# Turning the residual for the MLP: three of four column blocks by VectorE and device memory instead of TensorE

## The reference

```
x = x + mix @ w_out                       # w_out 2048 x 2048
u = relu(rms_norm(x, norm2_g) @ w_up)     # w_up  2048 x 8192
return x + square(u) @ w_down             # w_down 8192 x 2048
```

## Time and profile before

| | us |
|---|---|
| median of 3 runs (lowest, highest) | 1754.01 (1753.78, 1754.36) |
| the profiled execution's own time | 1757.45 |
| its span, first to last instruction | 1755.6 |
| PE busy | 1744.9 (99%) |
| DVE, ACT, POOL busy | 898.7, 669.1, 207.1 |

### The profile page before, as it was taken

One profiled execution on the slowest core, in us unless ns is written; L12 is line 12 of the kernel. 1 busy time (PEld: TensorE's weight loads), 2 busy tenths in 40 slices (PEclk: granted clock), 3 DMA queues, 4 the chain that ended last, 5 costly groups with the idle time before them and its releaser, 6 DMA issues.

```text
span 1755.6 us, 27160 instructions
## 1 busy us (share of the span) xinstructions
PE 1744.9 (99%) x9270; PEld 1582.7 (90%) x9270; DVE 898.7 (51%) x1718; ACT 669.1 (38%) x1256; POOL 207.1 (12%) x286
## 2 busy tenths in 40 slices
PE   9999999999999999999999999999999999999999
PEld 7999998899997789999888999888999888999887
DVE  5634776666677645454344454344444334545333
ACT  5323754444354444333332333333333333333332
POOL 3301010002352210110000110000111000111000
PEclk9999999999999999999999999999999999999999
DMA  7675469998798554444344444334443434444442
GB/s 182 189 181 149 122 163 222 197 202 217 198 258 261 152 142 115 125 121 130 121 131 120 128 122 123 129 124 127 121 130 120 131 120 130 121 122 129 141 147 96
DMA packets 381393, 261.54 MB, mean 149 GB/s; under 512 B 92444, under 2 KB 328156, under 8 KB 381324
## 3 DMA queue, kind: packets, MB, share of 16 engines
q1 hardware_dynamic: 353190, 222.09, 45.1%
q0 software_dynamic: 13072, 34.68, 7.6%
q10 hardware_dynamic: 15062, 3.86, 1.1%
HBM read 244.90 MB, written 21.46 MB: 152 GB/s over the span
## 4 chain that ended last, share of the span: by engine, by line
PE 96%; DVE 2%; SPq 1%; DMA 1%; issue 0%; ACT 0%; ACTq 0%; DVEq 0%
PE acc L520 18%; PE acc L521 18%; PE acc L522 17%; PE bank L607 8%; PE bank L608 8%; PE bank L606 8%; PE bank L1895 3%; PE ssb L606 2%; PE ssb L607 2%; PE ssb L608 2%; PE ssb L1895 1%; PE bank L566 1%; PE bank L567 1%; PE bank L565 1%; SPq L874 1%; PE acc L565 1%
## 5 line engine op out<-in xcount | busy, mean ns | idle before, releaser
L500 DVE TENSOR_TENSOR w_lo<-raw,w_hi 128x512 fp32r<-128x512 f32 x768 | 556.6, 733 | 780.5 <-ACT w_hi L491 779.9
L491 ACT ACTIVATE w_hi<-raw 128x512 fp32r<-128x512 f32 x768 | 482.2, 630 | 830.4 <-PE acc L522 402.6
L521 PE MATMUL acc<-x2g_lo,w_hi 128*128 128x384 f32 x1024 | 348.0, 340 | 0.0
L520 PE MATMUL acc<-x2g_hi,w_hi 128*128 128x384 f32 x1024 | 345.8, 338 | 0.0
L522 PE MATMUL acc<-x2g_hi,w_lo 128*128 128x384 f32 x1024 | 344.6, 337 | 0.0
L520 PE MATMUL acc<-a_hi,w_hi 128*128 128x400 f32 (+1 forms) x768 | 268.1, 349 | 0.2 <-DVE w_lo L500 0.2
L521 PE MATMUL acc<-a_lo,w_hi 128*128 128x400 f32 (+1 forms) x768 | 262.9, 342 | 0.0
L522 PE MATMUL acc<-a_hi,w_lo 128*128 128x400 f32 (+1 forms) x768 | 262.3, 342 | 0.0
L607 PE MATMUL bank<-w_lo,a_hi 128*128 128x512 f32 x640 | 253.0, 395 | 0.0
L608 PE MATMUL bank<-w_hi,a_lo 128*128 128x512 f32 x640 | 252.6, 395 | 0.0
L606 PE MATMUL bank<-w_hi,a_hi 128*128 128x512 f32 x640 | 252.0, 394 | 0.0
(11 more groups left out here) (339 smaller groups left out, 1517.0 us busy)
## 6 DMA issues: line engine op xcount, KB each, us to landing
raw<-in_w_up SPq DMA_DIRECT2D x128, 512.0 KB, 4.0
raw<-in_w_down SPq DMA_DIRECT2D x128, 512.0 KB, 3.7
raw<-in_w_in SPq DMA_DIRECT2D x94, 512.0 KB, 4.6
raw<-in_w_out SPq DMA_DIRECT2D x32, 512.0 KB, 4.6
vc<-in_cache_v POOLq DMA_DIRECT2D x32, 256.0 KB, 6.8
kc<-in_cache_k SPq DMA_DIRECT2D x128, 64.0 KB, 3.1
state_blocks<-in_state_C POOLq DMA_DIRECT2D x16, 256.0 KB, 4.5
C_blk<-state_blocks SPq DMA_DIRECT2D x4, 1024.0 KB, 8.9
```

Source lines behind the costliest of these rows:

```text
L491: e.activation(w_hi[:, q], raw[:, slot, 4 * (q % 2):4 * (q % 2) + 4, :], ACT.Copy).then_inc(hi_ready, 1)
L500: e.tensor_tensor(w_lo[:, q], raw[:, slot, 4 * (q % 2):4 * (q % 2) + 4, :], w_hi[:, q].bitcast(F32), ALU.subtract).then_inc(lo_ready, 1)
L520: e.matmul(out, w_hi[:, q, kk], hi[:, k, at], start=k == 0, stop=False, skip_group_check=True)
L521: e.matmul(out, w_hi[:, q, kk], lo[:, k, at], start=False, stop=False, skip_group_check=True)
```

## The change

Blocks 0 to 2 (k = 0 to 11) are no longer turned by TensorE. After the three additions of such a block, DVE turns it in 32 x 32 blocks into `stage` (`turn_blocks`, three instructions of 128 x 512). POOL then writes it to device memory so that the 32 x 32 blocks come to stand in their turned places (12 DMAs of 64 KB, in pieces of 128 bytes), waits until all 12 have landed, and reads it back, a feature on each partition, into one half of `m1` (one DMA of 768 KB, in pieces of 1536 bytes). ACT and DVE make `x2g_hi` and `x2g_lo` from `m1` instead of from PSUM, and later than before: block 0 in quarters 0 and 2 of tile 60, block 1 in quarters 0 and 2 of tile 62, block 2 in quarters 2 and 3 of tile 63. Block 3 stays as it was. `mm_out`'s wait for a free bank becomes a wait for additions.

```diff
@@ constants
+Y_TURNS = (1, 2, 0)
+X2_BLOCKS = 3
@@ mm_out, free(k, r): when a bank may be written again
-                    e.wait_ge(S("x2_lo_made"), 4 * (c - 1))
+                    e.wait_ge(S("y_added"), 12 + 3 * (c - 1))
@@ x2_due(t, q)
-            n = 4 * (t - T_OUT2 - 2) + q - 1
-            k = 4 * (n // 8) + n % 8
-            return (k, k + 1) if 0 <= n < 24 and n % 8 in (0, 2) else ()
+            return {(T_OUT2 + 4, 0): (0, 1), (T_OUT2 + 4, 2): (2, 3), (T_OUT2 + 6, 0): (4, 5), (T_OUT2 + 6, 2): (6, 7),
+                    (T_MLP - 1, 2): (8, 9), (T_MLP - 1, 3): (10, 11)}.get((t, q), ())
@@
+        x2_blocks = stage[:].rearrange("p j t -> p (j t)")[:, 0:3 * 4 * P]
+        def x2_part(k):
+            if k < 4 * X2_BLOCKS:
+                return m1[:, k % 8, 0:3 * P]
+            return x2_bank(k)[:, LIVE]
+        def x2_there_for(e, k):
+            if k < 4 * X2_BLOCKS:
+                e.wait_ge(S("x2_landed"), 16 * (k // 4 + 1))
+            else:
+                e.wait_ge(S("x2_turned"), k - 4 * X2_BLOCKS + 1)
@@ POOL, after the eight stores of new_keys and ahead of the two memsets
+            for c in range(X2_BLOCKS):
+                e.wait_ge(S("x2_blocks_made"), 3 * (c + 1))
+                for a in range(4):
+                    rows = slice(32 * a, 32 * a + 32)
+                    for r in range(3):
+                        dma(bass.AP(tensor=x2_turned_d.tensor, offset=c * 4 * P * 3 * P + P * r + 32 * a,
+                                    ap=[[3 * P, 32], [32 * 3 * P, 16], [1, 32]]),
+                            x2_blocks[rows, 4 * P * r:4 * P * (r + 1)], "x2_stored")
+                e.wait_ge(S("x2_stored"), 16 * 12 * (c + 1))
+                if c == 0:
+                    e.wait_ge(S("mix_lo_made"), 16)
+                elif c == 2:
+                    e.wait_ge(S("x2_lo_made"), 4)
+                dma(m1[:, 4 * (c % 2):4 * (c % 2) + 4, 0:3 * P], x2_turned_d[c].rearrange("(k p) t -> p k t", p=P),
+                    "x2_landed")
@@ ACT, new_x: x2g_hi
-                    e.wait_ge(S("x2_turned"), k + 1)
-                    e.activation(x2g_hi[:, k, LIVE], x2_bank(k)[:, LIVE], ACT.Copy,
+                    x2_there_for(e, k)
+                    e.activation(x2g_hi[:, k, LIVE], x2_part(k), ACT.Copy,
@@ DVE, add_out: after the additions of half 1
+                if half and c < X2_BLOCKS:
+                    turn_blocks(c)
+            def turn_blocks(c):
+                if c == 0:
+                    for j in range(2):
+                        e.wait_ge(S(f"spilled{j}"), 16 * 8)
+                else:
+                    e.wait_ge(S("x2_stored"), 16 * 12 * c)
+                e.wait_ge(S("y_added"), Y_OUT // 2 + 3 * c + 3)
+                for n, r in enumerate(Y_TURNS):
+                    e.transpose(x2_blocks[:, 4 * P * n:4 * P * (n + 1)],
+                                y_rows[:, r, 4 * c * P:4 * (c + 1) * P]).then_inc(S("x2_blocks_made"), 1)
@@ DVE, new_x: x2g_lo
-                    stt(x2g_lo[:, k, LIVE], x2_bank(k)[:, LIVE], g2[:, k:k + 1], x2g_hi[:, k, LIVE].bitcast(F32),
+                    stt(x2g_lo[:, k, LIVE], x2_part(k), g2[:, k:k + 1], x2g_hi[:, k, LIVE].bitcast(F32),
@@ TensorE, new_x
+                    if k < 4 * X2_BLOCKS:
+                        continue
                     e.wait_ge(S("y_added"), Y_OUT // 2 + 3 * (k // 4) + 3)
-                    if k % 4 == 3:
-                        e.wait_ge(S("x2_lo_made"), k - 2 if k < KT - 1 else 12)
```

More of the change, by code:

```diff
@@ L289, in build @@
         new_keys = nc.dram_tensor("new_keys", [4, 8, 13 * 32, 32], F32).ap()
+        x2_turned_d = nc.dram_tensor("x2_turned", [X2_BLOCKS, 4 * P, 3 * P], F32).ap()
         state_blocks_d = nc.dram_tensor("state_blocks", [P, BD * NH, DV], F32).ap()
```

## The result

| | runs | median, us (lowest, highest) |
|---|---|---|
| before | 8 | 1754.16 (1753.78, 1755.20) |
| after | 8 | 1760.10 (1759.05, 1761.34) |

The ratio is 1.0035, 95% interval 1.0026 to 1.0043: the changed kernel is slower by 5.9 us. The profiled execution took 1760.89 us with a span of 1758.8.

A forecast was written before the change was run, and what follows sets the result against it. The prediction took TensorE, busy for 99% of the span, to bound the kernel. On the median of 1754.01 us, -4.0 for transposes, +6.3 for the stop and +1.6 for the clock gave +3.9, 1757.9 us; range 1749.9 to 1763.

The forecast's parts named there:

- The likeliest case: Block 2 lands late, TensorE stops and its clock falls: +3.9 us, 1757.9 us, chance 0.42.
- Transposes saved: 36 of TensorE's 48 transposes go, six groups at 0.66 us each: 4.0 us less.
- The trip of block 2: From its last addition through turning, 12 stores, last landing and load: 2.1 + 7.2 + 2.5 + 6.5 = 18.3 us.
- the issue price of 0.65: POOL's time per store issue, in us; the twelfth store would start 7.2 us after the first.
- The chain behind the landing: Work on ACT and DVE listed behind the wait for block 2, through block 3's additions: 5.4 us.
- What was allowed: Longest round trip of block 2 that would not stop TensorE before block 3's transposes: 12.0 us.
- The stop: TensorE stands ahead of block 3's transposes, from 674.96 until 681.3: 6.3 us of new idle time.
- The clock: After the stop TensorE may restart at its lower clock, 1.2 GHz: 1.6 us for one cold start.
- Blocks 0 and 1: Their round trips, needed in tiles 60 and 62, would land in time, each with 2.7 us to spare.
- The rival with more than one block late: POOL's queue stands still after `new_keys` stores, delaying block 0, or trips exceed 21 us: +8.1, 1762.1 us, chance 0.21.
- The rule on one DMA: 2.0 us plus bytes at 436 GB/s: load 3.8, last store 2.0, round trip 15.1 us, time 1753.1 us.
- the landing of the last store: The last of a block's twelve stores lands 2.5 us after its start, bounds 1.9 and 5.8.

The follow-up runs named there:

- experiment 5: Changed kernel with each block stored by 4 DMAs of 192 KB in place of 12 of 64 KB, still in 128-byte pieces: 1758.38 us, ratio 1.0026.
- experiment 4: Changed kernel with 8 calls multiplying constants, read by nothing, to fill TensorE's stop ahead of block 3's transposes: 1758.07 us, ratio 1.0023.
- experiment 7: Changed kernel with four stores per block, written in pieces of 6 KB in place of 128 bytes (output wrong): 1754.30 us, ratio 1.0000.
- experiment 1: Changed kernel with only two blocks sent through device memory and the third turned by TensorE: 1751.83 us, ratio 0.9989.
- experiment 6: Changed kernel with four stores per block and block 2's parts made in tile 64's quarter 0, behind block 3's additions: 1751.78 us, ratio 0.9991.

## Why the prediction held, and where its terms were off

The likeliest case came about by its own mechanism, block 2 late and the clock down; +3.9 us were forecast and +5.9 measured. Point by point:

- **Transposes saved**: 4.0 forecast, 3.65 found. The price of a group was 0.61 and not 0.66.
- **The trip of block 2**: 18.3 forecast, 19.5 found, with two misses that partly cancel, which is luck. The load went out 5.2 us after the last store's start and not 2.5, and it took 4.9 and not 6.5. The median of four stores of 32 KB in a quiet stretch was the wrong row for the last of twelve of 64 KB; the upper end kept for it, 5.8, was nearer. The turning (1.9 for three, plus the way to POOL) and the issue price of 0.65 were right, but experiment 5 shows that the issue was not the limit which the step took it to be: with half the issue time the trip's store part got only 1.2 us shorter.
- **The chain behind the landing**: 5.4 forecast, 5.3 found, by the instructions and in the order named.
- **What was allowed**: 12.0 forecast; found 671.87 - 5.33 - 654.36 = 12.2.
- **The stop**: 6.3 forecast, 7.3 found; that is the longer trip, 1.2 us, less those 0.2.
- **The clock**: 1.6 forecast, 2.0 by times (experiment 4) and 2.8 by the trace. The row at the program's start gave too little: a loss of 1.6 us is some 3 us of work at half pace, and here the lower level lasted for 6 us after work began again. The 3.3 us at the end of the span in which the clock stayed up told nothing of such a stop: experiment 7 stood for 2.4 us and lost it. The Trainium skill, TensorE: Matmul & The Clock Gate, Why this matters for your kernels, had warned of it, and the trace now agrees: 1.00 before the stop, 0.50 after.
- **Blocks 0 and 1**: no stop of TensorE, as forecast. ACT waited 1.61 and 0.69 us for their loads in tiles 60 and 62, where next to nothing was forecast, but inside the 2.7 us to spare, and TensorE was busy for all 20 us of 640 to 660.
- **The rival with more than one block late** did not come about. POOL's queue stood still again between its two sets of `new_keys`, 11.23 us where it was 11.04, but not ahead of block 0's stores: they waited 4.08 us for DVE, and 0.78 in their midst for nothing shown (POOL's timeline).

```profile
613.77 5.44 POOL L657 DMA_DIRECT2D out<-new_keys  x4 [11.23 <-issue]
623.29 3.88 POOL L657 DMA_DIRECT2D x_turned<-stage  x6 [4.08 <-DVE stage L1646]
627.95 3.85 POOL L657 DMA_DIRECT2D x_turned<-stage  x6 [0.78 <-issue]
```

- **The rule on one DMA** (the Trainium skill, DMA: Bandwidth & Descriptors, Anatomy of one DMA): the estimates by it, 3.8 us for the load and 2.0 for the last store, stand against 4.9 and 5.2 in this trace. By them the time would have been 1753.1; the measurement decides against them here, beside a stream of weights.

So no step of the path failed, though one reason given for it, the issuing as what sets the trip, did not hold. Three terms were mis-sized, all to the same side: 0.35 us too much for the transposes, 1.0 too little for the stop, 1.2 too little for the clock. They are the 2.6 us between the forecast of +3.9 and the trace's +6.5. The largest single miss, 2.7 us on the landing of the last store, was more than half covered by the load, so that +3.9 came nearer than the terms deserved.

## What to carry to other kernels

A transfer that takes the place of work on the busiest engine has to be priced against the time that each of its uses has to spare, one by one: here the same 19 to 20 us were free for two blocks and cost 6 us for the third, and moving two blocks (experiment 1) is 8 us better than moving three in the same way. Ask what stands behind a wait in its engine's list: what came late to TensorE were additions that needed nothing of the late block, and listing them ahead of the wait halved the stop. A stop of TensorE can cost more than its length, 1.7 to 2.8 us here by the traces, as the clock falls; the short stops in experiment 6's profile did not cost that.

## What the runs showed of the hardware that was not expected

- Fewer and larger stores hardly landed sooner: for block 2 the four of 192 KB take 6.3 us each to land (median), where the twelve of 64 KB take 4.0. Over the three blocks, the 768 KB in pieces of 128 bytes are stored after 10 to 11 us the one way and after 12 the other. The profile's rows on block 2's DMA issues (656 to 670), from the changed kernel and from experiment 5:

```profile
x_turned<-stage POOLq DMA_DIRECT2D x12, 64.0 KB, 4.0
```

```profile
x_turned<-stage POOLq DMA_DIRECT2D x4, 192.0 KB, 6.3
```

- A short stop can be enough for the clock to fall, and the lower level lasts into the work behind it. In experiment 7, windows of the stop and of what follows:

```profile
671.70:674.00 2.30, 0.00 (x0) 0.00 (x0) 2.30 (x5) 0.75 (x2) 0.00 (x0) 1.00 0.50 142
674.05:677.00 2.95, 2.95 (x14) 2.95 (x15) 2.51 (x5) 1.84 (x4) 0.00 (x0) 0.51 0.32 89
678.00:680.00 2.00, 2.00 (x13) 2.00 (x12) 0.14 (x1) 0.59 (x2) 0.00 (x0) 1.00 0.37 111
```

The clock fell as work began again after 2.4 us without a matmul. It was back before 678 here, some 3 to 4 us into the work; in the changed kernel it took 6. The two stops of at most 0.5 us in experiment 6 left it at 1.00. But it does not fall in every execution of experiment 7: three of its ten runs have a mean granted clock of 1.000 and took 1752.31 to 1753.39 us, the seven at 0.999 took 1753.98 to 1755.52. The medians of the two sets are 2.0 us apart, near the 1.7 that the trace gives for the clock in this kernel. How long the stop was in the three is not on record, nor is why the return takes 3 us in one kernel and 6 in another.
